# A wait for VectorE's low weights is taken off GpSimd's subtractions in the second layer's expert combination

## The chip, the cores and the metric

The kernel runs on one core of a Trainium2 chip. The metric is the device time of one execution in microseconds, the lower the better.

## What is computed

The reference is a two-layer diffusion block over 512 latent and 256 context tokens of width 1024 (MLA and gated linear attention in the first layer, a gated linear recurrence in the second). Each layer ends in a PEER feed-forward: 8 heads pick 16 of 16,384 experts for every token, and each expert is one row of a table `u` and one row of a table `v`.

```
idx = top 16 of the 16 x 16 candidates of a head;  g = softmax(top_s)
act = gelu(einsum('td,thkd->thk', h, u[idx]))
out = einsum('thk,thkd->td', g * act, v[idx])
```

The kernel computes the first part of the tokens densely: it multiplies all experts' activations with gates that are zero for experts not chosen, and then this weight matrix with the whole table `v` (the "second products"). One tile of 128 tokens is left to gathers of single rows of `v` and sums on VectorE.

## The kernel before

`combine_with_dots` makes the second products of the second layer. The table has 128 slices of 128 experts; a group is four slices (`GC = 4`), and there are 32 groups (`NG`), two in each turn of a hardware loop. Of each slice a group needs the table rows `vr` (128 x 1024, float32), the activations `ar` (128 x 384) and the gates `gr`. float32 precision is had from float16 operands: a value is split into a high part (its cast) and a low part (what the cast lost), and three products high x high, low x high and high x low are summed in PSUM (`three_products`). The parts lie in double buffers (`q` and `1 - q`), `vr`, `ar` and `gr` in single ones.

The engines work as follows, each in its own written order:

- SyncE loads `gr` of a group when the group before is weighed, `ar[x]` when the low weights that read it are made, and `vr[x]` when the low row that reads it is made, in this order for x = 0 to 3.
- ScalarE (`casts`, L2009 and L2011) casts table row 0, weights 0, row 1, weights 1 and so on: `vh` as soon as the row has landed, `wh` when VectorE has weighed. It waits for the end of the group before last on PE, whose buffer it writes.
- VectorE (`period`) goes through the six pieces of the current group on PE (three token tiles by two halves of 512 columns). For each it adds the piece from PSUM into `ACC` (L2069). After piece 0 it copies the gather indices and weighs the following group's four slices (`weigh`, L2043: `ar` times `gr`); after pieces 1 and 2 it makes two low weights each (`low_weight`, L2048: `ar` minus `wh`). From piece 2 on it makes the shares (L2054) and one row sum each for pieces 2 to 5 (`add_row`, L2061: a gathered row times its share, added in PSUM).
- GpSimd, also Pool (`period`) makes the four low rows of the following group (`low`, L1979: `vr` minus `vh`), and then issues four gathers of table rows (`gather`, L1973). Each gather waits for the row sum that reads its buffer. Ahead of the lows stands the wait that the change takes out, for all four low weights of the following group. The first group's lows stand outside of `period` and have no such wait.
- PE (L2034) waits for the group's four low rows (`v_cut`) and four low weights (`w_cut`), then makes its six pieces, 72 matmuls, into six PSUM banks.

Semaphores count up over the whole stage. `w_cut` begins at 4, so that `g * GC + (2 * GC + 4)` is reached when the last low weight of group g + 1 is made.

Of the kernel before, what the change touches and what calls it, by code (L numbers as in the profile page):

```python
# [1915 lines left out]
def combine_with_dots(nc, io, gates, acts, chosen_rows, chosen_gates, dots, ACC, layer, first_tile, mods, early):  # L1916
# [4 lines left out]
    GC = 4  # L1921
# [8 lines left out]
    with ExitStack() as c:  # L1930
# [16 lines left out]
        with signals(nc, *names) as sems:  # L1947
# [6 lines left out]
            with nc.Block() as block:  # L1954
                @block.sync
                def _(sp):
                    with sp.Fori(0, NG) as g:
                        sp.wait_ge(weighed, g * GC + GC)
                        sp.dma_start(gr.rearrange("p n a t -> p n (a t)"),
                                     gates[first_tile:TILES - 1, :, bass.ds(g * GC, GC), :].rearrange("n b a t -> b n (a t)")).then_inc(g_in, 16)  # L1960
                        for x in range(GC):
                            s = g * GC + x
                            sp.wait_ge(w_cut, s + 1)
                            sp.dma_start(ar[x][:, :], acts[bass.ds(s, 1), :, 0:NT].rearrange("o p t -> p (o t)")).then_inc(a_in[x], 16)
                            sp.wait_ge(v_cut, s + 1)
                            sp.dma_start(vr[x][:, :], v_src[bass.ds(s, 1)].rearrange("o p d -> p (o d)")).then_inc(v_in[x], 16)
                    load_norm_rows(sp, io, mods, early["vec"], range(len(early["vec"])), early["vec_in"], layer, 1)

                @block.gpsimd
                def _(pool):  # L1970
                    def gather(rows, ring, x, q, done):
                        pool.sem_inc(issuing, 1)
                        nc.gpsimd.indirect_dma_start(ring[x][:, :], None, rows,  # L1973
                                                     bass.IndirectOffsetOnAxis(ap=index[q][:, x:x + 1], axis=0)).then_inc(done[x], 16)

                    def low(g, q, x):
                        pool.wait_ge(v_high, g * GC + (x + 1))
                        pool.wait_ge(second_done, g * NP + NP)
                        nc.gpsimd.tensor_tensor(vl[q][:, x, :], vr[x][:, :], vh[q][:, x, :], ALU.subtract).then_inc(v_cut, 1)  # L1979

                    def period(g, q):
                        pool.wait_ge(w_cut, g * GC + (2 * GC + 4))
                        for x in range(GC):
                            low(g + 1, 1 - q, x)
                        pool.wait_ge(index_set, g + 2)
                        for x in range(SLOTS):
                            pool.wait_ge(summed, g * SLOTS + (x + 1))
                            gather(v_rows, vg, x, 1 - q, vg_in)

                    pool.sem_inc(v_cut, 4)  # L1990
                    for x in range(GC):
                        low(0, 0, x)
                    pool.wait_ge(index_set, 1)
                    for x in range(SLOTS):
                        gather(v_rows, vg, x, 0, vg_in)
                    with pool.Fori(0, NG // 2 - 1) as it:
                        period(it * 2, 0)
                        period(it * 2 + 1, 1)
                    period(NG - 2, 0)

                @block.scalar
# [514 lines left out]
```

## Time and profile before

| | |
|---|---|
| median of 3 runs | 4840.32 us (4834.79 to 4843.66) |
| the profiled execution | 4828.37 us |
| its span, first to last instruction | 4826.6 us |
| granted TensorE clock, mean | 0.931 |
| busy in the span | PE 4176.4 us (87%), VectorE 3255.2 (67%), ScalarE 1554.4 (32%), Pool 1722.2 (36%) |
| the stage of the change | matmuls from 4154.3 to 4785.0 us |
| its 768 high x high matmuls | 308.5 us busy, 118.8 us of PE idle before them |
| its 128 low rows on Pool | 269.3 us busy, 234.3 us of Pool idle before them |

A time in a timeline is counted from the start of the span. The idle time in front of an instruction is put down to what ended it, which need not be what lasted longest. VectorE's consecutive instructions overlap by about 0.08 us in the records, so their spacing is a little under their duration.

### The profile page before, as it was taken

How to read it: one execution, taken by the hardware profiler on the slowest of the kernel's cores; microseconds unless marked ns; L12 is line 12 of the kernel's file. 1: busy time of each engine (PE TensorE's matmuls, PEld its weight loads, DVE VectorE, ACT ScalarE, POOL GpSimd, SP SyncE). 2: the span in 40 equal slices, each digit the busy share in tenths (PEclk: the TensorE clock that was granted, in tenths of full speed). 3: DMA queues.
4: the chain of work that ended last, by engine and by line, in shares of the span. 5: the costliest groups of instructions: out<-in, count | busy, mean ns of one | idle time of the engine just before them, and what ended most of it. 6: DMA issues, size and time to landing. Idle time of an engine off the chain costs nothing. (4 is left out here: it accounts for less than half of the span.)

```text
span 4826.6 us, 73515 instructions
## 1 busy us (share of the span) xinstructions
PE 4176.4 (87%) x23716; PEld 2270.7 (47%) x23716; DVE 3255.2 (67%) x10439; ACT 1554.4 (32%) x1963; POOL 1722.2 (36%) x1191
## 2 busy tenths in 40 slices
PE   5979777889999999799999987977898889688885
PEld 1546563556556555344444423434465546233332
DVE  2035535156787778788888875842899999466666
ACT  0014320024444444222222214821444434232221
POOL 0400002421111111466666632106344444466665
PEclk8989888899999999899999998988899999899998
DMA  5100231256886887799999961213789998888885
GB/s 210 52 23 4 72 103 38 86 140 166 237 225 173 225 233 201 270 346 349 342 342 348 341 232 54 78 57 97 219 250 311 280 320 260 288 298 293 291 289 185
DMA packets 374797, 1004.81 MB, mean 208 GB/s; under 512 B 35024, under 2 KB 121872, under 8 KB 367248
## 3 DMA queue, kind: packets, MB, share of 16 engines
q1 hardware_dynamic: 208188, 522.43, 32.1%
q0 software_dynamic: 101376, 318.81, 23.3%
q10 hardware_dynamic: 64996, 160.55, 8.8%
q8 instruction: 132, 2.16, 0.2%
q14 instruction: 105, 0.86, 0.0%
HBM read 804.43 MB, written 146.90 MB: 197 GB/s over the span
## 5 line engine op out<-in xcount | busy, mean ns | idle before, releaser
L1352 PE MATMUL ca_A<-hh,ca_uh 128*128 128x512 f16 (+2 forms) x3072 | 793.8, 313 | 94.1 <-DMA ca_ul<-ca_ur 77.1
L1352 PE MATMUL ca_A<-hl,ca_uh 128*128 128x512 f16 (+2 forms) x3072 | 792.4, 312 | 0.0
L1352 PE MATMUL ca_A<-hh,ca_ul 128*128 128x512 f16 (+2 forms) x3072 | 791.7, 312 | 0.0
L1313 POOL DMA_DIRECT2D ca_ul<-ca_ur x192 | 173.1, 901 | 984.4 <-ACT ca_ul L1385 955.3
L1837 PE MATMUL ex_R<-ex_vh,ex_wh 128*128 128x512 f16 x1280 | 486.2, 380 | 29.2 <-DVE ex_wl L1851 29.2
L1837 PE MATMUL ex_R<-ex_vl,ex_wh 128*128 128x512 f16 x1280 | 486.1, 380 | 0.0
L1837 PE MATMUL ex_R<-ex_vh,ex_wl 128*128 128x512 f16 x1280 | 486.1, 380 | 0.0
L2034 PE MATMUL ex_R<-ex_vh,ex_wh 128*128 128x512 f16 x768 | 308.5, 402 | 118.8 <-POOL ex_vl L1979 86.0
L1352 PEld LDWEIGHTS ca_A<-hh,ca_uh 128*128 128x128 f16 x3072 | 261.2, 99 | 282.6 <-issue 59.0
L1768 POOL TENSOR_TENSOR ex_vl<-ex_vr,ex_vh 128x1024 f16<-128x1024 f32 x128 | 270.9, 2149 | 257.7 <-DVE ex_wl L1851 222.0
L1393 ACT ACTIVATE ca_ga<-ca_A 128x640 f32<-128x640 f32 (+1 forms) x256 | 152.8, 597 | 651.6 <-PE ca_A L1352 585.6
L1979 POOL TENSOR_TENSOR ex_vl<-ex_vr,ex_vh 128x1024 f16<-128x1024 f32 x128 | 269.3, 2136 | 234.3 <-DVE ex_wl L2048 192.8
L1352 PEld LDWEIGHTS ca_A<-hh,ca_ul 128*128 128x128 f16 x3072 | 261.3, 99 | 194.7 <-issue 11.9
L1352 PEld LDWEIGHTS ca_A<-hl,ca_uh 128*128 128x128 f16 x3072 | 261.4, 99 | 190.3 <-issue 11.0
L1537 DVE TENSOR_SCALAR ca_hot<-ca_iota,ca_cur 128x128 f16<-128x128 f16 (+1 forms) x1024 | 340.4, 333 | 0.0
L1536 DVE TENSOR_SCALAR ca_hot<-ca_iota,ca_cur 128x128 f16<-128x128 f16 (+1 forms) x1024 | 329.2, 322 | 4.5
L1383 ACT ACTIVATE ca_uh<-ca_ur 128x1024 f16<-128x1024 f32 x256 | 269.4, 1053 | 130.3 <-ACT ca_ga L1393 50.5
L1497 DVE SCALAR_TENSOR_TENSOR ca_match<-ca_iota,ca_best,ca_ci 128x64 f32<-128x64 f16 x1280 | 307.5, 308 | 2.3
L2034 PE MATMUL ex_R<-ex_vl,ex_wh 128*128 128x512 f16 x768 | 308.4, 402 | 0.0
L2034 PE MATMUL ex_R<-ex_vh,ex_wl 128*128 128x512 f16 x768 | 307.7, 401 | 0.0
L1878 DVE TENSOR_TENSOR ACC<-ACC,ex_R 128x512 f32<-128x512 f32 x320 | 219.1, 685 | 113.8 <-PE ex_R L1837 112.3
L2069 DVE TENSOR_TENSOR ACC<-ACC,ex_R 128x512 f32<-128x512 f32 x192 | 131.7, 686 | 217.4 <-PE ex_R L2034 217.1
(371 smaller groups left out, 8095.4 us busy)
## 6 DMA issues: line engine op xcount, KB each, us to landing
ca_ur<-in_peer_u SPq DMA_DIRECT2D x256, 512.0 KB, 4.9
ex_vr<-in_peer_v SPq DMA_DIRECT2D x256, 512.0 KB, 4.6
gates<-ca_stage ACTq DMA_DIRECT2D x32, 2048.0 KB, 10.9
ca_ul<-ca_ur POOLq DMA_DIRECT2D x192, 256.0 KB, 5.2
acts<-ca_ga ACTq DMA_DIRECT2D x128, 320.0 KB, 3.6
ex_gr<-gates SPq DMA_DIRECT2D x32, 1280.0 KB, 7.8
ex_ar<-acts SPq DMA_DIRECT2D x128, 320.0 KB, 6.0
acts<-ca_ga ACTq DMA_DIRECT2D x128, 192.0 KB, 5.2
```

The source lines that it names most:

```text
L1313: nc.gpsimd.dma_start(ul[j][:, :, :].rearrange("p k n -> p (k n)"), ur[j][:, :, :].rearrange("p k n -> p (k n)"), accum_op=ALU.add).then_i ...
L1352: last = nc.tensor.matmul(A[b][:, a:a + w], lhs[j][:, k, :], rhs[:, k, a:a + w], start=(k == 0 and x == 0), stop=(k == KD - 1 and x == 2))
L1383: nc.scalar.activation(uh[j][:, :, :], ur[j][:, :, :], ACT.Copy).then_inc(u_split, 1)
L1393: nc.scalar.activation(ga[b][:, :], A[b][:, 0:NT], ACT.Gelu).then_inc(gelu_done, 1)
L1497: step.mark(nc.vector.scalar_tensor_tensor(match[:, k, :], iota[:, 0:CAND], posf[:, h, k:k + 1], ci[:, h, :], ALU.is_equal, ALU.mult, accu ...
L1536: nc.vector.tensor_scalar(hot[j][:, x, 0, :], row[:, :], w(0), None, ALU.is_equal)
L1537: last = nc.vector.tensor_scalar(hot[j][:, x, 1, :], row[:, :], w(1), w(2), ALU.is_equal, ALU.mult)
L1768: nc.gpsimd.tensor_tensor(vl[q][:, x, :], vr[x][:, :], vh[q][:, x, :], ALU.subtract).then_inc(v_cut, 1)
L1837: last = nc.tensor.matmul(R[(NP * q + y) % BANKS][:, :], lhs[q][:, x, o:o + P], rhs[q][:, x, h * 512:h * 512 + 512], start=(x == 0 and n = ...
L1878: nc.vector.tensor_tensor(part, part, R[(NP * q + y) % BANKS][:, :], ALU.add).then_inc(added, 1)
L1979: nc.gpsimd.tensor_tensor(vl[q][:, x, :], vr[x][:, :], vh[q][:, x, :], ALU.subtract).then_inc(v_cut, 1)
L2034: last = nc.tensor.matmul(R[(NP * q + y) % BANKS][:, :], lhs[q][:, x, o:o + P], rhs[q][:, x, h * 512:h * 512 + 512], start=(x == 0 and n = ...
```

## The change

GpSimd's wait for the four low weights of the following group is taken out of `combine_with_dots`. The four low rows then wait for their own casts and for PE alone. The order of instructions on every engine stays.

```diff
                     def period(g, q):
-                        pool.wait_ge(w_cut, g * GC + (2 * GC + 4))
                         for x in range(GC):
                             low(g + 1, 1 - q, x)
                         pool.wait_ge(index_set, g + 2)
```

The waits that stay in `low`:

```python
                        pool.wait_ge(v_high, g * GC + (x + 1))
                        pool.wait_ge(second_done, g * NP + NP)
```

## Rows read from the trace of the kernel before

**Rows 1.** Windows of stretches: busy time of each engine, granted clock, DMA share.

```profile
4198.00:4768.00 570.00, 492.73 (x2089) 211.19 (x2089) 370.37 (x580) 163.24 (x231) 353.49 (x233) 0.93 0.85 293
...
2000.00:2100.00 100.00, 99.94 (x464) 45.13 (x462) 87.55 (x124) 26.01 (x35) 62.56 (x46) 1.00 0.97 364
```

**Rows 2.** Waits of the stage, from 4150 to 4790.

```profile
POOL ex_vl L1979 <- DVE ex_wl L2048: 192.8, 30, 7.1
...
PE ex_R L2034 <- POOL ex_vl L1979: 86.0, 31, 6.1
```

**Rows 3.** PE's timeline: starts of four groups.

```profile
4177.73 0.60 PE L2034 MATMUL ex_R<-ex_vh,ex_wh 128*128 128x512 f16 x1 [6.06 <-POOL ex_vl L1979]
...
4433.79 0.39 PE L2034 MATMUL ex_R<-ex_vh,ex_wh 128*128 128x512 f16 x1 [2.67 <-POOL ex_vl L1979]
...
4453.86 0.39 PE L2034 MATMUL ex_R<-ex_vh,ex_wh 128*128 128x512 f16 x1 [2.68 <-POOL ex_vl L1979]
...
4767.99 0.39 PE L2034 MATMUL ex_R<-ex_vh,ex_wh 128*128 128x512 f16 x1 [2.49 <-POOL ex_vl L1979]
```

**Rows 4.** VectorE's timeline: one group and the last add.

```profile
4438.27 0.69 DVE L2069 TENSOR_TENSOR ACC<-ACC,ex_R 128x512 f32<-128x512 f32 x1 [5.23 <-PE ex_R L2034]
...
4438.95 1.96 DVE L2043 TENSOR_TENSOR ex_ar<-ex_ar,ex_gr 128x384 f32<-128x384 f32 x4
...
4441.47 1.02 DVE L2048 TENSOR_TENSOR ex_wl<-ex_ar,ex_wh 128x384 f16<-128x384 f32 x2
4443.45 0.69 DVE L2069 TENSOR_TENSOR ACC<-ACC,ex_R 128x512 f32<-128x512 f32 x1 [0.96 <-PE ex_R L2034]
...
4785.43 0.69 DVE L2069 TENSOR_TENSOR ACC<-ACC,ex_R 128x512 f32<-128x512 f32 x1 [0.70 <-PE ex_R L2034]
```

**Rows 5.** Pool's timeline: the lows of that group.

```profile
4445.35 8.39 POOL L1979 TENSOR_TENSOR ex_vl<-ex_vr,ex_vh 128x1024 f16<-128x1024 f32 x4 [6.86 <-DVE ex_wl L2048]
```

**Rows 6.** ScalarE's timeline: casts of table rows.

```profile
4166.88 1.06 ACT L2009 ACTIVATE ex_vh<-ex_vr 128x1024 f16<-128x1024 f32 x1 [2.69 <-DMA ex_vr<-in_peer_v]
...
4439.97 1.04 ACT L2009 ACTIVATE ex_vh<-ex_vr 128x1024 f16<-128x1024 f32 x1
...
4441.33 1.04 ACT L2009 ACTIVATE ex_vh<-ex_vr 128x1024 f16<-128x1024 f32 x1
```

**Rows 7.** Timelines of Pool and VectorE, first group.

```profile
4143.36 2.12 POOL L1979 TENSOR_TENSOR ex_vl<-ex_vr,ex_vh 128x1024 f16<-128x1024 f32 x1 [30.01 <-ACT ex_vh L2009]
...
4144.54 1.36 DVE L2043 TENSOR_TENSOR ex_ar<-ex_ar,ex_gr 128x384 f32<-128x384 f32 x1 [1.23 <-DMA ex_ar<-acts]
...
4150.24 2.43 POOL L1979 TENSOR_TENSOR ex_vl<-ex_vr,ex_vh 128x1024 f16<-128x1024 f32 x1
4150.62 2.47 DVE L2048 TENSOR_TENSOR ex_wl<-ex_ar,ex_wh 128x384 f16<-128x384 f32 x1
```

**Rows 8.** Timelines of Pool and VectorE, second group.

```profile
4169.22 8.39 POOL L1979 TENSOR_TENSOR ex_vl<-ex_vr,ex_vh 128x1024 f16<-128x1024 f32 x4 [11.44 <-PE ex_R L2034]
...
4169.22 1.29 DVE L2061 SCALAR_TENSOR_TENSOR ex_sum<-ex_vg,ex_share,ex_sum 128x1024 f32<-128x1024 f32 x1 [0.21 <-DVE ex_share L2054]
...
4171.02 1.28 DVE L2061 SCALAR_TENSOR_TENSOR ex_sum<-ex_vg,ex_share,ex_sum 128x1024 f32<-128x1024 f32 x1
...
4174.60 1.28 DVE L2061 SCALAR_TENSOR_TENSOR ex_sum<-ex_vg,ex_share,ex_sum 128x1024 f32<-128x1024 f32 x1
```

**Rows 9.** Timelines of VectorE and Pool, the stage before: gathers and what follows them.

```profile
3600.02 0.07 DVE L1463 DVE_READ_ACCUMULATOR ca_ug<-ca_ug,ca_hp 128x1 f32 x1
...
3600.90 0.96 POOL L1327 DMA_INDIRECT ca_ug<-in_peer_u_rows,chosen_rows  x1 [4.10 <-DVE ca_ug L1463]
...
3608.43 0.96 POOL L1327 DMA_INDIRECT HS<-in_peer_u_rows,chosen_rows  x1 [0.30 <-issue]
3609.38 2.16 POOL L1317 TENSOR_TENSOR ca_ul<-ca_ur,ca_uh 128x1024 f16<-128x1024 f32 x1
```

**Rows 10.** DMA issues on the page: name, queue, count, size, us to landing.

```profile
ex_vr<-in_peer_v SPq DMA_DIRECT2D x256, 512.0 KB, 4.6
```

## The prediction

> **What bounds the kernel now.** I went from the page to the one stage that the diff touches, and then into one of its groups. The windows view [rows 1] shows the steady stretch: PE busy 86%, VectorE 65%, Pool 62%, ScalarE 29%, DMA share 0.85 at 293 GB/s. No engine is full, so a cycle of waits sets the pace. The waits view [rows 2] names it: Pool's subtractions (the lows) wait for VectorE's low weights (wl), 192.8 us in 30 waits, and PE for the lows, 86.0 us in 31. PE's starts of the second group and of the last lie 590.26 us apart for 30 groups [rows 3]: 19.68 us each.
>
> The reader is to see the cycle in the timelines of the group that starts on PE at 4433.79 [rows 3]. VectorE adds piece 0 at 4438.27, having stood idle for 5.23 us, weighs four times, adds piece 1, makes wl0 and wl1, waits 0.96 us for piece 2, adds it at 4443.45 and makes wl2 and wl3 [rows 4]. Only then, at 4445.35, do the four lows begin, 8.39 us in a row [rows 5]; PE waits 2.68 us for the last and starts the next group at 4453.86 [rows 3]. So the group is 11.56 us up to the lows, 8.39 us of lows and 0.12 us of handover: 20.07 us. (The mean is below that since some groups are shorter.)
>
> **The change part by part.** One wait goes, on Pool, once a group, 31 times. Nothing is added and nothing is computed otherwise. Each low still waits for ScalarE's cast of its row and for the end of the group before on PE.
>
> What is late next. ScalarE has cast row 0 long before, but its order is row, weights, row, weights, so the cast of row 1 stands behind the first cast of weights, and this behind weighing 0; row casts then come every 1.36 us [rows 6] and a low takes 2.12 us [rows 7], so the casts get ahead. Pool's own order is the other gate: its fourth gather of a group waits for VectorE's fourth row sum, the last thing that VectorE does in a group, and low 0 of the next group is queued behind that gather. Pool and VectorE therefore begin a group together, and all four lows fall into the part in which VectorE weighs and makes wl.
>
> There lies the cost. In the stage's first group, where the removed wait does not stand, they already run beside those VectorE instructions [rows 7]. A weighing that meets a low takes 1.36 us and a wl 2.47 us, where one alone takes 0.55 (four weighings 1.96, two wl 1.02 [rows 4]); both end 0.42 us after the low that they met. Low 0 ends at 4145.48 and low 3 at 4152.67: 2.40 us from end to end, not 2.12. So VectorE gets exactly one such instruction in between two lows; there were four such meetings, all alike. Instructions with an operand in PSUM aren't held: the row sum at 4174.60, inside the lows that ran from 4169.22 to 4177.61 [rows 8], takes 1.28 us like the others.
>
> VectorE's work with nothing in its way, from start to start: add 0 and index 0.67, four weighings 1.91, add 1 0.61, two wl 0.94, add 2 0.61, two wl 0.94 [rows 4]; share 0.27 (0.18, and 0.36 with its wait), three row sums with an add each 5.38, last row sum 1.19 [rows 8]. The sum is 12.5 us.
>
> Now the walk, with zero at add 0; the last row sum of the group before ends at 0.1. A gather starts 0.81 us after the VectorE instruction that it waits for has ended (3600.09 to 3600.90), takes 0.96 us, and a Pool subtraction follows it at once [rows 9]. So low 0 asks at 1.9. The weighings start at 0.67, 1.15, 1.63 and 2.10. Low 0 gets in behind the third and ends at 4.17. The fourth is held and VectorE goes on at 4.51 (1.93 lost). Add 1 is free; wl0, from 5.12, is held by low 1 until 6.57, next at 6.91 (1.32 lost). wl1 is held by low 2 until 8.97, next at 9.31 (1.93 lost). Add 2 is free; wl2, from 9.92, is held by low 3 until 11.37, next at 11.71 (1.32 lost). wl3 ends at 12.26. Lost in all: 6.5 us, so VectorE's group is 12.5 + 6.5 = 19.0 us.
>
> PE starts its next group at about 12.4 and needs 17.44 us up to the last add (4767.99 to 4785.43 [rows 3, 4], with its slow start), so it is ready in time: VectorE is the bound. I take 19.1 us, for the loop's branch, which no idle time hides any more. Nothing in the trace prices it; the bounds are nothing and the 0.21 us that VectorE idles behind the share [rows 8].
>
> The first group: the cast of row 3 starts at 4166.88 since its table row lands late [rows 6], so low 3 runs from 4168.0 to 4170.1 and holds wl2; VectorE goes on at 4170.5 with wl3, share, 5.38 and 1.19, and reaches add 0 of the second group at 4177.8. (Bounds: 2 us either way, the price of one meeting.) PE's second group starts where the first ends, 6.06 us before 4177.73 [rows 3], and is no limit.
>
> PE's last group then starts at 4177.8 + 29 x 19.1 + 12.4 = 4744.1, where it now starts at 4767.99. **The sum: 23.9 us less.** PE's last 17.44 us and the closing norm stay. Against the profiled execution's 4828.37 us (span 4826.6) that is 4804.5. The median of the runs shown, 4840.32, is 0.25% above it, so the forecast is 4840.3 - 23.9 = 4816 us.
>
> Bounds. If low 0 asks before 1.6, it gets in behind the second weighing, the third and fourth are both held for 1.93, and the same walk gives 19.6: 9 us less in all. If it asks behind the fourth, 19.0 again. Break-even is 19.9. Operands: a table row's load is issued as its low ends, the last at about 12, and lands in 4.6 us at the median [rows 10]; it is wanted more than 10 us after it is issued, so it costs nothing; the other bound is the late landing of the first group, 2 us once more. DMA would have to move a group's 5.75 MB (293 GB/s x 19.66 us) at 302 GB/s, and another stage moves 364 [rows 1].
>
> The Trainium skill has a rule that speaks against this change (SBUF — State Buffer, "Who interferes with whom"): a VectorE instruction with two SBUF inputs and a GpSimd instruction that reads SBUF contend for a shared port, the one that starts first keeps it to its end and the other blocks fully. The trace agrees on what is held and what isn't [rows 7, 8]. The rule doesn't say who is next when both want it: by it alone the group could be the 19.0 us of turns or the 20.8 us of rival 2.
>
> **The rivals.**
> 1. Low 0 asks early, or small overheads on VectorE add up: 19.5 to 19.9 us a group, 0 to 12 us less, 4834 in the middle. For it: the 0.81 us comes from another stage's gathers, and everything on VectorE now counts. Against: the same instruction on the same queue.
> 2. Slower: Pool keeps the port from low to low. The fourth weighing is then held from 2.10 until all lows are done at 10.5, and the group is 10.8 + 10.0 = 20.8 us; PE starts its last group at 4177.8 + 29 x 20.8 + 14.1, 27 us later than now: 4867. It decides from 19.9 us on, that is, when VectorE loses two of its turns in a group. For it: the next low is ready at once. Against: every meeting in [rows 7].
> 3. Much faster: meetings cost little, since lows slip among adds and row sums. PE would be the bound at 15.5 us (72 matmuls at 0.215, without idle or slow start) or DMA at 5.75 MB / 364 GB/s = 15.8: 29 x 3.9 = 113 us less, 4727. Against: the gather ties low 0 to the end of VectorE's group, so lows and weighings meet every time.
> 4. The wait gives nothing away, since another takes its place: casts, or late table rows, hold the lows. Then nothing moves by more than 9 us: 4840; or it costs some more, if loads now land on each other. Against: in the walk the casts are 1.4 to 3.4 us ahead of lows 1 to 3.
>
> **Chances.** Forecast (18.9 to 19.3 us a group, 17 to 30 us less) 0.56; rival 1 0.17; rival 2 0.09; rival 3 0.07; rival 4 0.11. Some 0.2% (9.7 us) is what a measurement of this kernel can tell from no change. Faster: 0.54 + 0.06 of rival 1 + 0.07 = 0.67. Slower: 0.09 + 0.05 of rival 4 = 0.14. Same: what is left, 0.19. The forecast's own range is 4808 to 4826. For 8 in 10 the range takes in rivals 1 and 4 above, and below a few meetings that fall out: 4796 to 4848. Rivals 2 and 3 are left out.
>
> **What would show it.** VectorE's busy share of the steady stretch goes from 65% to over 95%; Pool's lows have a mean near 2.35 us and end 2.4 us apart; wl has a mean near 1.7 us and weighing near 1.0, and row sums keep 1.28. PE's wait at a group's start is some 1.6 us and is put down to wl, not to the lows. It is wrong if lows still wait long for something (rival 4), if groups come under 18 us apart (rival 3), or if one VectorE instruction of 8 us stands in each (rival 2). What can most easily make the forecast wrong is who gets the port, and the moment at which low 0 asks.

## The result: slower, and the profile after

The changed kernel takes 4853.78 us (median of 11 runs, 4847.77 to 4860.39), the kernel before, beside it on the same chip, 4837.79 us (11 runs, 4833.4 to 4843.66). The ratio is 1.0033, with a 95% interval of 1.0023 to 1.0042: slower, by 16 us or 0.33%. I had forecast 24 us less; 4853.78 lies above my range too, which ended at 4848. The profiled execution took 4850.3 us, its span is 4848.5 us.

The windows view of the steady stretch after the change (columns as in [rows 1]):

```profile
4198.00:4768.00 570.00, 482.62 (x2013) 205.40 (x2011) 566.74 (x557) 161.11 (x224) 358.06 (x224) 0.92 0.76 281
```

VectorE was busy for 65% of this stretch and is now for 99.4% (566.74 of 570). DMA share fell from 0.85 to 0.76 and PE did less, 2013 recorded matmuls against 2089: VectorE is the bound, and the pace is lower than before. The waits view of the stage, from 4150 to 4812:

```profile
ACT ex_wh L2010 <- DVE ex_ar L2042: 245.2, 57, 8.4
...
PE ex_R L2033 <- DVE ex_wl L2047: 129.8, 32, 32.3
POOL ex_vl L1979 <- ACT ex_vh L2008: 55.6, 29, 2.1
```

Pool's wait for VectorE's low weights, 192.8 us [rows 2], is gone, as the diff says. In its place PE waits for the low weights, and ScalarE for weighings. Where VectorE spends its time is seen in its timeline of one group, from add 0 to the next add 0 (two views: the first shows the four weighings merged into one line, the second the third weighing alone):

```profile
4427.79 0.68 DVE L2068 TENSOR_TENSOR ACC<-ACC,ex_R 128x512 f32<-128x512 f32 x1
...
4428.46 8.57 DVE L2042 TENSOR_TENSOR ex_ar<-ex_ar,ex_gr 128x384 f32<-128x384 f32 x4
4436.95 0.68 DVE L2068 TENSOR_TENSOR ACC<-ACC,ex_R 128x512 f32<-128x512 f32 x1
4437.55 1.01 DVE L2047 TENSOR_TENSOR ex_wl<-ex_ar,ex_wh 128x384 f16<-128x384 f32 x2
...
4439.08 2.34 DVE L2047 TENSOR_TENSOR ex_wl<-ex_ar,ex_wh 128x384 f16<-128x384 f32 x2
...
4448.10 0.68 DVE L2068 TENSOR_TENSOR ACC<-ACC,ex_R 128x512 f32<-128x512 f32 x1
```

```profile
4429.40 7.16 DVE L2042 TENSOR_TENSOR ex_ar<-ex_ar,ex_gr 128x384 f32<-128x384 f32 x1
```

And Pool's timeline of the same group:

```profile
4428.69 1.13 POOL L1973 DMA_INDIRECT ex_vg<-in_peer_v_rows,ex_index  x1 [0.85 <-DVE ex_sum L2060]
4429.84 6.29 POOL L1979 TENSOR_TENSOR ex_vl<-ex_vr,ex_vh 128x1024 f16<-128x1024 f32 x3
4438.14 2.40 POOL L1979 TENSOR_TENSOR ex_vl<-ex_vr,ex_vh 128x1024 f16<-128x1024 f32 x1 [2.00 <-ACT ex_vh L2008]
```

The third weighing starts in the records at 4429.40 and ends at 4436.56, 0.43 us after the last of three lows that follow one another without a pause. It isn't given a turn between them. It is freed only when Pool stops by itself: low 3 needs the cast of its row, ScalarE's cast stands behind the casts of weights, and those wait for the held weighing. Low 3 then meets one wl, which takes 1.87 us. So a group loses 7.16 - 0.55 = 6.6 us and 1.87 - 0.54 = 1.3 us, and is 20.31 us from add 0 to add 0, where I had walked to 19.0. The next group is the same but for 0.16 us more (20.47), and the two lengths alternate. 26 of the 31 groups with a run of lows look like this.

In four groups Pool's last gather ends later, all four weighings and with them the casts are over by then, and one wl is held through all four lows; such a group lasts 20.9 to 21.1 us. (The fifth exception is the first group.) VectorE's and Pool's timelines of such a group:

```profile
4267.16 9.11 DVE L2047 TENSOR_TENSOR ex_wl<-ex_ar,ex_wh 128x384 f16<-128x384 f32 x1
```

```profile
4264.91 2.54 POOL L1973 DMA_INDIRECT ex_vg<-in_peer_v_rows,ex_index  x1 [0.85 <-DVE ex_sum L2060]
4267.47 8.37 POOL L1979 TENSOR_TENSOR ex_vl<-ex_vr,ex_vh 128x1024 f16<-128x1024 f32 x4
```

PE's timeline, starts of the second group, of one in the middle and of the last, as in [rows 3]:

```profile
4175.83 0.39 PE L2033 MATMUL ex_R<-ex_vh,ex_wh 128*128 128x512 f16 x1 [0.33 <-DVE ex_wl L2047]
...
4441.66 0.60 PE L2033 MATMUL ex_R<-ex_vh,ex_wh 128*128 128x512 f16 x1 [3.12 <-DVE ex_wl L2047]
...
4790.11 0.60 PE L2033 MATMUL ex_R<-ex_vh,ex_wh 128*128 128x512 f16 x1 [3.18 <-DVE ex_wl L2047]
```

The 30 groups take 614.28 us, 20.48 each, where they took 19.68: 24.0 us more. The first group lasts from 4157.96 to 4175.83, 17.87 us, where it took 4177.73 - 4154.27 = 23.46: 5.6 us less. The stage began 3.7 us later, ahead of anything that the diff touches (in the profiled executions of the experiments it began anywhere from 4154.4 to 4171.3). 24.0 - 5.6 + 3.7 = 22.1, and the spans differ by 21.9 us.

### The profile page after: what moved, and what is told of

Read it like the earlier page. It is cut to its first block and busy times, and to the rows that moved or that the text cites. A ratio compares the mean times of both kernels' runs of the same rounds, so it can differ in the third digit from the quotient of the medians.

```text
span 4848.5 us, 73485 instructions
## 1 busy us (share of the span) xinstructions
PE 4181.9 (86%) x23716; PEld 2273.8 (47%) x23716; DVE 3483.1 (72%) x10439; ACT 1556.8 (32%) x1963; POOL 1741.0 (36%) x1191
## 5 line engine op out<-in xcount | busy, mean ns | idle before, releaser
L1878 DVE TENSOR_TENSOR ACC<-ACC,ex_R 128x512 f32<-128x512 f32 x320 | 219.1, 685 | 113.8 <-PE ex_R L1837 112.2
L2042 DVE TENSOR_TENSOR ex_ar<-ex_ar,ex_gr 128x384 f32<-128x384 f32 x128 | 238.3, 1919 | 11.8 <-DMA ex_ar<-acts 11.8
```

What stands on the lines that cost most here:

```text
L1878: nc.vector.tensor_tensor(part, part, R[(NP * q + y) % BANKS][:, :], ALU.add).then_inc(added, 1)
L2042: nc.vector.tensor_tensor(by_tile(ar[x]), by_tile(ar[x]), gr[:, :, x, :], ALU.mult).then_inc(weighed, 1)
```

## The experiments

Each starts from the changed kernel and edits `combine_with_dots` alone. Where several runs were timed the ratio has an interval; a single time can be off by some 10 us, and is read with its trace. The stage alone, from its first matmul to the start of its last add, lasted 631.2 us before and 649.4 after the change; in the experiments 639.3 (1), 609.2 and 607.9 (2, two launches), 622.5 (3), 499.9 (4), 648.5 (5), 556.1 (6), 671.8 (7), 638.1 (8) and 624.6 (9).

**1. Lows 1 to 3 wait for the low before them.** It opens a gap between two lows and changes no order.

```diff
                         for x in range(GC):
+                            if x:
+                                pool.wait_ge(v_cut, g * GC + (2 * GC + x))
                             low(g + 1, 1 - q, x)
```

> The changed kernel, but each of the lows 1 to 3 also waits for the low before it to have ended, a wait on Pool's own work. Theory A (Pool keeps the port from low to low because its next low is already waiting when one ends): the own wait leaves a gap at each end, the held weighing comes free after low 0, weighings have a mean near 1.0 us instead of 1.92, lows last 2.4 us, groups are about 19.0 to 19.5 us apart: 27 to 42 us less than the changed kernel's 4854. Theory B (what counts is when VectorE's instruction arrives: one that is already waiting when the first low starts is passed over until Pool itself stops): nothing changes but the gaps, groups 20.4 us or a few tenths more, 4854 to 4865.

Measured: 4844.77 us (9 runs, 4836.66 to 4853.44), ratio to before 1.002 (1.0009 to 1.003). VectorE's timeline, then Pool's:

```profile
4501.57 3.02 DVE L2044 TENSOR_TENSOR ex_ar<-ex_ar,ex_gr 128x384 f32<-128x384 f32 x1
...
4504.51 2.48 DVE L2044 TENSOR_TENSOR ex_ar<-ex_ar,ex_gr 128x384 f32<-128x384 f32 x1
```

```profile
4502.02 2.15 POOL L1979 TENSOR_TENSOR ex_vl<-ex_vr,ex_vh 128x1024 f16<-128x1024 f32 x1
4504.39 2.19 POOL L1979 TENSOR_TENSOR ex_vl<-ex_vr,ex_vh 128x1024 f16<-128x1024 f32 x1 [0.22 <-PE ex_R L2035]
```

The third weighing is released in a gap of 0.22 us and ends 0.42 us after low 0, where it was held for 7.16 us. (The view names PE as what ended the gap; the only wait that the edit adds is the one on Pool's own low.) From there every meeting costs one low: 2.5, 1.9, 1.3 and 1.9 us are lost, 7.6 in all, for 20.1 us a group. Neither of the two expected lengths came. The gap gives VectorE its turns back, but the third weighing is still held, which my walk had let through; hence 20.1 and not 19.0.

**2. Low 0 waits for two weighings** of the group that follows, at the place of the removed wait. Timed in a second launch.

```diff
                     def period(g, q):
+                        pool.wait_ge(weighed, g * GC + (2 * GC + 2))
                         for x in range(GC):
```

> The changed kernel with a wait of the lows for the first two of the four weighings of their group: low 0 no longer starts right behind the gather but while weighing 2 runs, and weighing 3 arrives inside low 0. Theory B (arrival decides): VectorE gets its turn after each low, weighings have a mean near 1.0 us, groups 19.0 to 19.3 us apart. Theory A (Pool keeps the port whenever its next low is ready): weighing 3 is held through all four lows, some 8.5 us in one instruction, group 20.7 us.

> The kernel that waits for two weighings, timed in rounds: 19.05 us a group as in its profile, which is 0.6 us less than the kernel before in 30 groups and 6 us less in the first: 4811 to 4818 beside 4836, ratio 0.995 to 0.997.

Measured: 4812.36 us in the first launch (a single run), 4814.17 (4 runs, 4804.61 to 4816.15) in the second, ratio 0.9945 (0.9929 to 0.9962). VectorE's timeline of the first launch (the two weighings before these start at 4490.79 and 4491.26), and Pool's:

```profile
4492.19 2.54 DVE L2043 TENSOR_TENSOR ex_ar<-ex_ar,ex_gr 128x384 f32<-128x384 f32 x1
...
4495.25 1.89 DVE L2048 TENSOR_TENSOR ex_wl<-ex_ar,ex_wh 128x384 f16<-128x384 f32 x1
...
4497.06 2.48 DVE L2048 TENSOR_TENSOR ex_wl<-ex_ar,ex_wh 128x384 f16<-128x384 f32 x1
```

```profile
4491.01 1.13 POOL L1973 DMA_INDIRECT ex_vg<-in_peer_v_rows,ex_index  x1 [0.85 <-issue]
4492.17 9.36 POOL L1979 TENSOR_TENSOR ex_vl<-ex_vr,ex_vh 128x1024 f16<-128x1024 f32 x4
```

This is my walk, step by step: the third weighing gets through, the fourth, wl0, wl1 and a third wl are held by one low each, 2.0 + 1.3 + 1.9 + 1.3 = 6.6 us are lost (forecast: 6.5), and a group is 18.96 us from add 0 to add 0 (4490.12 to 4509.08). The four lows stand back to back here too, 9.36 us instead of 8.4, since VectorE gets in between them. So the arithmetic of turns was right, and back-to-back lows alone don't lock VectorE out.

**3. Low 0 waits for all four weighings.** The same line with `g * GC + 3 * GC`.

> The changed kernel with a wait of the lows for all four weighings of their group, instead of the removed wait for its four low weights. Weighings are never held (0.55 us). Theory B (arrival decides): wl0 arrives inside low 0, VectorE has a turn after each low, wl has a mean near 2.1 us, groups are 19.1 us apart: about 4815, under both kernels. Theory A (Pool keeps the port): wl0 is held through all four lows, 8.5 us in one instruction, group 20.5 us, about 4856.

Measured: 4827.61 us (10 runs, 4821.83 to 4835.79), ratio 0.999 (0.998 to 0.9999). That is 13 us above the 4815 expected: groups are 19.3 and 19.5 us in turn, and not 19.1, since all four wl are held (6.9 us lost), and the first group took 25.6 us. Lows begin 0.84 us after the gather has ended and take turns with all four wl, two of which are shown:

```profile
4500.11 2.28 DVE L2048 TENSOR_TENSOR ex_wl<-ex_ar,ex_wh 128x384 f16<-128x384 f32 x1
...
4502.31 2.48 DVE L2048 TENSOR_TENSOR ex_wl<-ex_ar,ex_wh 128x384 f16<-128x384 f32 x1
```

**4. Pool writes and doesn't read.** The low rows are filled with zeros: the low part of the table rows is left out of the result, and a Pool instruction takes 0.96 us instead of 2.12, so this also shortens Pool's work.

```diff
-                        nc.gpsimd.tensor_tensor(vl[q][:, x, :], vr[x][:, :], vh[q][:, x, :], ALU.subtract).then_inc(v_cut, 1)
+                        pool.sem_inc(issuing, 1)
+                        nc.gpsimd.memset(vl[q][:, x, :], 0.0).then_inc(v_cut, 1)
```

> The changed kernel with each low row's subtraction replaced by a memset of the same tile, which reads nothing (the low parts of the table are left out as zeros, and a low is shorter, about 0.9 us). If it is the reading of SBUF by Pool that holds VectorE, weighings and wl all take 0.55 us and VectorE's group falls to 12.5 us, so that PE or the DMA is the bound at 15.5 to 17 us a group. If any Pool instruction holds VectorE, weighings or wl still show held ones of over 1 us.

Measured: 4697.24 us (a single run). The windows view of its steady stretch, and timelines of VectorE and Pool:

```profile
4198.00:4650.00 452.00, 452.00 (x2096) 204.90 (x2095) 372.56 (x581) 161.01 (x228) 218.29 (x231) 1.00 0.99 369
```

```profile
4502.16 1.96 DVE L2043 TENSOR_TENSOR ex_ar<-ex_ar,ex_gr 128x384 f32<-128x384 f32 x4
```

```profile
4502.53 0.96 POOL L1980 MEMSET ex_vl<- 128x1024 f16 x1
```

```profile
4502.10 1.43 DVE L2051 COPY ex_index<-chosen_rows 128x4 int32 x1
4502.16 1.36 DVE L2043 TENSOR_TENSOR ex_ar<-ex_ar,ex_gr 128x384 f32<-128x384 f32 x1
...
4505.50 0.56 DVE L2048 TENSOR_TENSOR ex_wl<-ex_ar,ex_wh 128x384 f16<-128x384 f32 x1 [0.26 <-ACT ex_wh L2011]
```

```profile
4505.23 0.95 POOL L1980 MEMSET ex_vl<- 128x1024 f16 x1 [1.73 <-ACT ex_vh L2009]
```

The plain case is the second write: a wl begins and ends inside it and takes 0.56 us, as alone. The first write, from 4502.53 to 4503.49, falls among four weighings. They take 1.96 us together, as alone, so no time is lost. But the index copy's record lasts 1.43 us there and the first weighing's 1.36, both ending just after the write, and by my own criterion (a weighing of over 1 us) that is a held one. A gather stands ahead of this write and overlaps both records; what lengthens them isn't settled. PE is never idle in this stretch, and is the bound at 15.5 us a group, the figure of my rival 3. So 20.48 - 15.5 = 5 us a group go with Pool's subtractions. The edit takes away their reads and 1.16 us of each at once, so the share of the reads alone isn't shown. DMA moves 369 GB/s without being late.

**5. Low 0 waits for one weighing.** The line of experiment 2 with `2 * GC + 1`.

> As the kernel that waits for two weighings, but for the first weighing alone; this one is over before the gather ahead of low 0 has ended, so the wait holds nobody back. Theory (the VectorE instruction that is issued before low 0 starts is passed over by back-to-back lows): weighing 2 is held through lows 0 to 2 again, some 7.2 us, weighings have a mean of 1.9 us, groups are 20.4 us apart, about 4853. Rival (a wait on VectorE's work between gather and lows is enough to get turns): 19.05 us a group, 4812, as with two weighings.

Measured: 4856.85 us (a single run), as without a wait. VectorE and Pool:

```profile
4495.73 0.55 DVE L2043 TENSOR_TENSOR ex_ar<-ex_ar,ex_gr 128x384 f32<-128x384 f32 x1
...
4496.67 7.16 DVE L2043 TENSOR_TENSOR ex_ar<-ex_ar,ex_gr 128x384 f32<-128x384 f32 x1
```

```profile
4495.96 1.14 POOL L1973 DMA_INDIRECT ex_vg<-in_peer_v_rows,ex_index  x1 [0.85 <-DVE ex_sum L2061]
4497.12 6.29 POOL L1979 TENSOR_TENSOR ex_vl<-ex_vr,ex_vh 128x1024 f16<-128x1024 f32 x3
```

Set this beside experiment 2. Low 0 starts 0.45 us after the third weighing here (4497.12 - 4496.67), and also there (4492.17 - 4491.72, the third weighing being the fourth's start less 0.47), and in both directly behind the gather. Here the third weighing is held for 7.16 us, there it passes and turns are taken. What differs is when low 0's wait is met: here at the end of the first weighing, 4496.28, that is 0.82 us before the gather ends at 4497.10; there at the end of the second, 4491.80, 0.34 us before the gather ends at 4492.14.

**6. VectorE weighs ahead of the pieces, with the removed wait put back.** A version for speed: the lows then fall into the row sums, which aren't held [rows 8].

```diff
-    weigh_at, low_at, sum_at = (0, 0, 0, 0), (1, 1, 2, 2), (2, 3, 4, 5)
+    low_at, sum_at = (0, 0, 1, 1), (2, 3, 4, 5)
...
                     def period(g, q):
+                        pool.wait_ge(w_cut, g * GC + (2 * GC + 4))
...
                         dve.wait_ge(added, g * NP + BANKS)
+                        for x in range(GC):
+                            if following:
+                                weigh(g + 1, x)
                         for y, (t, h) in enumerate(pieces):
...
-                                if weigh_at[x] == y and following:
-                                    weigh(g + 1, x)
-                            for x in range(GC):
```

> The wait of the kernel before is put back, and VectorE works further ahead instead: it weighs the following group's slices before the add of piece 0 and makes two low weights each after pieces 0 and 1. If the cycle low weights, lows, PE sets the pace of the kernel before, the lows start some 3 to 4 us earlier, beside the row sums that they don't hold: the last cast of weights comes at about 7.4 us after PE's start, the lows end at 16.6, groups are 16.7 to 17.5 us apart, 65 to 90 us less than the kernel before, 4745 to 4775. Rival (DMA or the table rows' landing is the bound at once): 18.5 us a group or more, over 4800.

Measured: 4764.03 us (4 runs, 4754.7 to 4768.59) against 4835.36 of before, ratio 0.9844 (0.9828 to 0.9861), the fastest version that computes everything. Its windows view, VectorE and Pool:

```profile
4198.00:4650.00 452.00, 420.25 (x1913) 185.62 (x1912) 372.18 (x528) 150.75 (x208) 329.89 (x211) 0.99 0.96 336
```

```profile
4503.80 1.88 DVE L2054 TENSOR_TENSOR ex_share<-dots,chosen_gates 128x4 f32 x1
4505.72 1.29 DVE L2061 SCALAR_TENSOR_TENSOR ex_sum<-ex_vg,ex_share,ex_sum 128x1024 f32<-128x1024 f32 x1
```

```profile
4503.54 8.39 POOL L1979 TENSOR_TENSOR ex_vl<-ex_vr,ex_vh 128x1024 f16<-128x1024 f32 x4 [3.88 <-DVE ex_wl L2048]
```

In this stretch weighings take 554 ns and low weights 550 ns at the mean, as alone; only the share meets a low, which costs it up to 1.8 us. PE is busy 93%, VectorE 82%, and a group is 17.2 us at the mean. The wait that the change took out for being long is what keeps the lows off VectorE's work; what made it long was that the low weights came late.

**7. The same order without the wait.** It also puts a weighing inside the run of lows instead of ahead of it, which tests whether the moment of arrival decides.

> The same order on VectorE, without the wait. Lows and low weights meet again; wl0 arrives inside low 0, so VectorE has its turns: 12.5 + 6.5 us on VectorE, groups 19.0 us apart, about 4813, and slower than with the wait. If the wait were what costs, this one would be the faster of the two, below 16.7 us a group.

Measured: 4878.64 us (a single run), the slowest of all. VectorE and Pool:

```profile
4509.59 7.31 DVE L2042 TENSOR_TENSOR ex_ar<-ex_ar,ex_gr 128x384 f32<-128x384 f32 x1 [2.31 <-DMA ex_ar<-acts]
```

```profile
4508.11 8.36 POOL L1979 TENSOR_TENSOR ex_vl<-ex_vr,ex_vh 128x1024 f16<-128x1024 f32 x4
```

The weighing comes 1.5 us after low 0 has begun, and is held until the last of the four lows has ended none the less. The theory that VectorE is passed over only if it was there before low 0, and with it my 19.0 us a group, fails: groups are 21.1 us. (The 2.31 us of waiting for the activations' load are a second cost of this order without the wait.)

**8. A gap behind low 0 alone.**

```diff
                         for x in range(GC):
+                            if x == 1:
+                                pool.wait_ge(v_cut, g * GC + (2 * GC + 1))
                             low(g + 1, 1 - q, x)
```

> The changed kernel; only low 1 waits for the low before it to have ended, lows 2 and 3 follow with no such wait. Theory C (how a run of lows begins decides: one that follows the gather at once passes VectorE over until Pool stops, one that begins after Pool has stopped lets VectorE in at each end): weighing 2 comes free after low 0 (3.0 us), then weighing 3, wl0 and wl1 have one turn each, lows 2 and 3 last 2.4 us, groups 20.1 us apart, as with own waits at all three. Theory D (passing over goes on in any back-to-back run of lows): weighing 3 is held through lows 1 to 3, some 7 us, lows last 2.13 us, groups 21 us apart, about 4872.

Measured: 4847.87 us (a single run), a group 20.04 us (adds at 4512.90 and 4532.94). VectorE and Pool:

```profile
4514.51 3.01 DVE L2044 TENSOR_TENSOR ex_ar<-ex_ar,ex_gr 128x384 f32<-128x384 f32 x1
...
4517.45 2.48 DVE L2044 TENSOR_TENSOR ex_ar<-ex_ar,ex_gr 128x384 f32<-128x384 f32 x1
...
4520.45 1.88 DVE L2049 TENSOR_TENSOR ex_wl<-ex_ar,ex_wh 128x384 f16<-128x384 f32 x1
```

```profile
4514.96 2.14 POOL L1979 TENSOR_TENSOR ex_vl<-ex_vr,ex_vh 128x1024 f16<-128x1024 f32 x1
4517.32 7.00 POOL L1979 TENSOR_TENSOR ex_vl<-ex_vr,ex_vh 128x1024 f16<-128x1024 f32 x3 [0.23 <-PE ex_R L2035]
```

One gap of 0.23 us is enough for the whole group. Lows 1 to 3 follow one another without a pause, 7.00 us against 6.29 for three such lows in the change, and VectorE gets in after each.

**9. The order of experiment 6 with a wait for the four weighings** (`pool.wait_ge(weighed, g * GC + 3 * GC)`) where experiment 6 waits for the low weights.

> VectorE in the order of the kernel that weighs first, with a wait of the lows for the four weighings only. Theory C: the wait ends after the gather's issue and the run of lows begins on it, so VectorE has a turn after each low: wl0 arrives inside low 0, wl has a mean near 2.2 us, groups 19.2 to 19.6 us apart, 4815 to 4830, against 21.7 us without this wait. Rival (in this order of VectorE the lows pass it over in any case): wl0 held through all four lows, groups over 20.5 us, over 4855.

Measured: 4832.73 us (a single run, beside 4834.78 of before); a group 19.29 us (adds 0 at 4509.07 and 4528.36). VectorE and Pool:

```profile
4509.67 1.89 DVE L2051 COPY ex_index<-chosen_rows 128x4 int32 x1
...
4511.94 2.48 DVE L2048 TENSOR_TENSOR ex_wl<-ex_ar,ex_wh 128x384 f16<-128x384 f32 x1
```

```profile
4509.40 9.40 POOL L1979 TENSOR_TENSOR ex_vl<-ex_vr,ex_vh 128x1024 f16<-128x1024 f32 x4 [0.37 <-ACT ex_vh L2009]
```

Against experiment 7 one wait is added, so that low 0 starts 0.37 us after its gather has ended. (The view names the cast of row 0, which had long ended; the fourth weighing ended 0.25 us before low 0.) With it the one instruction held for 7.31 us becomes four turns, which cost 1.7 us (the index copy), 1.9, 1.3 and 1.9 (three wl). The time is not far from that of experiment 3, as two kernels with nearly the same meetings should be (a little above the 4815 to 4830 expected, though the groups are as long as expected), and 68 us from experiment 6 (4764.81 us in its profiled execution), whose lows keep out of VectorE's way.

## Why the prediction was wrong

**What bounds the kernel; what is late next.** Right. The lows start as soon as the fourth gather is out, in the part in which VectorE weighs; low 0 came 2.05 us after add 0 (1.9 forecast). VectorE is the bound (99.4% busy, "over 95%" forecast), PE waits for wl (3.1 us a group, 1.6 forecast), and row sums keep 1.28 us. The other signs point at the failure below: weighings have a mean of 1.9 us (1.0 forecast), wl of 1.1 (1.7), and lows follow one another at 2.1 us and not 2.4.

**VectorE's own work, 12.5 us.** Right: 20.31 less 7.9 lost is 12.4, and in experiment 2 18.96 less 6.6 is 12.4. The 0.1 us that I added for the loop's branch, which nothing priced, is 0.16 us in every second group here, 0.08 a group, if that step is the branch: the loop has two groups a turn.

**The steps that failed: "Low 0 gets in behind the third and ends at 4.17", and "So VectorE gets exactly one such instruction in between two lows; there were four such meetings, all alike."** Both are about who gets in. The run of lows starts where I had put it, 0.44 us after the third weighing's record begins, but it is the third that is held (for 7.16 us) and not the fourth: the later record wins here. With turns from low 1 on this alone makes a group of 20.0 to 20.2 us (experiments 1 and 8), past the break-even of 19.9: the third weighing's meeting costs 2.5 us, where my bound of 19.6 had 1.93 for it. And VectorE gets no turn until Pool stops, which makes 20.48 of it. So of the 1.4 us a group between 19.1 and 20.48 some 1.0 is the first step and 0.4 the second. They come and go together: experiment 2, whose low 0 starts at the same place among the weighings, has neither, and gives 18.96 us a group and 4814 us where my walk had 19.0 to 19.1 and 4816. The four meetings [rows 7] were real, but all of one kind: Pool had waited 30.01 us for a cast before that run of lows, while in the change low 0 has its operands long before its gather ends.

**The first group.** Forecast: 6.06 us of PE's idle time less. Measured: 0.33 us idle left, the group 5.6 us shorter. Its second add 0 came 24.48 us after the stage's first matmul, 0.95 us later than forecast and inside the 2 us allowed. I had counted one meeting, of low 3 with a wl; there were two, since low 2 also held the fourth weighing (1.80 us).

**The rivals.** Rival 2 was the mechanism, and 0.09 was too little for it. I had put it at 20.8 us and 4867: about right for a group in which one instruction is held through four lows (20.9 to 21.1), too high for the usual one, in which the held weighing keeps back the cast of row 3 and so stops Pool after three lows (rival 4's cause, working in VectorE's favour). 20.48 us stand between, and 4853.78 too. My evidence against it, "every meeting", was four samples of another situation. Rival 3's price was right (15.5 us, experiment 4) for a kernel in which Pool only writes, and for a shorter time.

VectorE instructions with two SBUF inputs lost time beside Pool's subtractions, which read, and none beside its writes (a wl of 0.56 us inside a Pool write, experiment 4). The Trainium skill (SBUF — State Buffer, "Who interferes with whom") states the same two cases, and of two instructions that contend it says: "Whoever issues first gets the shared pair for the whole instruction". Read from the starts in the records, the runs don't bear this last rule out: the weighing recorded at 4429.40 lost to a low recorded at 4429.84. Whether a record's start is the moment of issue that the page means, no run shows.

**What decides between the two ways** is shown only as far as the runs go. VectorE was passed over where low 0's last wait was met 0.8 us or more before the gather in front of it ended (the change, experiments 5 and 7). Turns were taken where it was met 0.34 us before that end (experiment 2) or after it (experiments 3 and 9), and from the first gap in Pool's run on (experiments 1 and 8). The traces of experiments 2, 3 and 9 hold four groups that test this inside a single kernel. There the gather in front of low 0 ends later than in the others, so that low 0's wait had been met 3.3 us (experiment 2), 2.4 (3), 0.8 and 2.0 us (9) before that end, and one VectorE instruction is held through all four lows (9.10, 9.11, 8.73 and 8.63 us), while the groups around them take turns. VectorE's and Pool's timelines of the one in experiment 2 (the line of two wl holds the one of 9.10 us):

```profile
4704.23 9.57 DVE L2048 TENSOR_TENSOR ex_wl<-ex_ar,ex_wh 128x384 f16<-128x384 f32 x2
```

```profile
4703.30 1.23 POOL L1973 DMA_INDIRECT ex_vg<-in_peer_v_rows,ex_index  x1 [0.30 <-issue]
4704.55 8.36 POOL L1979 TENSOR_TENSOR ex_vl<-ex_vr,ex_vh 128x1024 f16<-128x1024 f32 x4
```

So the presence of the wait in the program doesn't decide; in which way a group goes follows its timing. Between 0.34 and 0.8 us nothing was measured. That the gathers take part, or how the engine lines up its next instruction, was not tried separately and stays open.

## What to carry to other kernels

- Before a wait between two engines goes, ask what it keeps apart. Here the lows fell beside row sums, which they don't hold; without the wait they fell beside weighings and low weights, which they do. Making the awaited work earlier (experiment 6, 71 us less) kept the wait and took away its length.
- A price read from a few meetings holds for the situation of those meetings: look how the run of instructions began, not only at the two that met. Where two ways of sharing are possible and the break-even lies between them (19.9 us here, between 19.0 and 20.8), the chance of the worse one is not small.
- If Pool's SBUF work must run beside VectorE's, a wait that is met just before the run, or one gap of 0.22 us in it, can bring the turns back: some 40 us lie between the change (4853.78) and experiment 2 (4814.17).

## What the runs showed of the hardware

- Back-to-back Pool subtractions can hold one VectorE instruction through all of them: 7.16 us through three, 7.31 us (arriving 1.5 us into the first) and 9.11 us through four. The lows aren't lengthened by it, 2.10 us from start to start. With turns they stand 2.4 us apart, three in 7.00 us and four in 9.36.
- The held instruction can be the one whose record starts first (4429.40 against 4429.84).
- A 128x4 index copy took 1.89 us beside a low and 0.16 alone, and 1.88 us were measured for the 128x4 share (0.15 alone): small instructions pay the rest of the low as large ones do.
- Pool's 128x1024 write of 0.95 us cost VectorE no time: a wl inside it took 0.56 us, and four weighings around another took 1.96 us together, though two records beside that one, right behind a gather, were long (1.43 and 1.36 us).
